# Issuing 22 small GpSimd DMAs of a two-layer trunk ahead of the constants instead of behind the fourth weight chunk

## The reference

```python
cs = silu(c)
for i in range(2):
    mod = cs @ w_mod[i] + b_mod[i]                      # 1024 x 6144: six vectors of 1024
    sh_m, sc_m, g_m, sh_f, sc_f, g_f = split(mod, 6)
    h = rmsnorm(x, norm_mix[i]) * (1 + sc_m) + sh_m
    y = hybrid_ab(h, ...) if i == 0 else multiscale_pool(h, ...)
    x = x + g_m * y
    h = rmsnorm(x, norm_ffn[i]) * (1 + sc_f) + sh_f
    x = x + g_f * hier_moe(h, w_gr[i], b_gr[i], w_er[i], b_er[i], w_gate[i], w_up[i], w_down[i])
return rmsnorm(x, norm_out)
```

## Time and profile before

| | |
|---|---|
| median of three executions | 904.04 us |
| the profiled execution | 904.04 us |
| its span, first to last instruction | 902.3 us |
| TensorE (PE) busy | 768.5 us, 85% |
| VectorE (DVE), ScalarE (ACT), GpSimd (POOL) busy | 242.9, 162.8, 37.0 us |
| mean granted TensorE clock | 0.906 of full |
| SP's DMA queue (q1) | 268.22 MB, 75.2% of 16 engines' span |
| GpSimd's DMA queue (q0) | 1.02 MB, 0.6% |

### The profile page before, as it was taken

How to read it: one execution, slowest core, us unless ns; L and a number is a source line. 1 busy time by engine, 2 the same in 40 slices (tenths; PEclk the granted TensorE clock), 3 DMA queues, 4 the chain that set the end, 5 groups by cost and what they waited for, 6 DMA issues and landing times.

```text
span 902.3 us, 9000 instructions
## 1 busy us (share of the span) xinstructions
PE 768.5 (85%) x3194; PEld 380.0 (42%) x3194; DVE 242.9 (27%) x667; ACT 162.8 (18%) x331; POOL 37.0 (4%) x63
## 2 busy tenths in 40 slices
PE   3799998697587899999999969965898999999994
PEld 1486676342452233333333326454532333333331
DVE  1105323611441212121222223525322121212124
ACT  2112022301122211111111102030311121212111
POOL 4600000000200000000000000001000000000000
PEclk9598998598588999999999986875999999999998
DMA  9977277016316999999999798555199999999961
GB/s 319 340 223 271 94 280 280 0 60 251 155 40 277 374 422 420 418 400 413 417 419 421 279 374 321 183 233 222 41 375 422 418 407 423 407 420 418 412 257 46
DMA packets 62138, 269.59 MB, mean 299 GB/s; under 512 B 3950, under 2 KB 6094, under 8 KB 37536
## 3 DMA queue, kind: packets, MB, share of 16 engines
q1 hardware_dynamic: 61152, 268.22, 75.2%
q0 software_dynamic: 960, 1.02, 0.6%
HBM read 268.18 MB, written 1.05 MB: 298 GB/s over the span
## 4 chain that ended last, share of the span: by engine, by line
PE 40%; issue 33%; DMA 18%; DVE 4%; ACT 3%; SPq 2%; POOL 1%; ACTq 0%; DVEq 0%; POOLq 0%
DMA ring<-in_w_up 14%; PE bank L673 7%; PE bank L483 5%; DMA ring<-in_w_mod 4%; PE bank L425 4%; PE bank L695 3%; PE bank L443 3%; PE bank L611 3%; PE bank L544 2%; PE bank L433 1%; PE bank L471 1%; PE bank L434 1%; PE bank L649 1%; PE bank L588 1%; PE bank L750 1%
## 5 line engine op out<-in xcount | busy, mean ns | idle before, releaser
L673 PE MATMUL bank<-ring,arena 128*64 128x512 f32 x1024 | 229.0, 600 | 30.6 <-DMA ring<-in_w_up 25.6
L673 PEld LDWEIGHTS bank<-ring,arena 128*64 128x64 f32 x1024 | 82.4, 138 | 156.9 <-issue 150.1
L709 PE MATMUL bank<-arena 128*128 128x512 f32 x256 | 117.9, 604 | 0.0
L695 PE MATMUL bank<-dn_w,hT 128*64 128x512 f32 x480 | 108.8, 593 | 0.6 <-DMA dn_w<-in_w_down 0.6
L1293 DVE SCALAR_TENSOR_TENSOR hT<-hT,bank 128x256 f32<-128x256 f32 x32 | 13.5, 421 | 235.8 <-ACT hT L936 235.8
L709 PEld LDWEIGHTS bank<-arena 128*128 128x128 f32 x256 | 46.2, 190 | 71.2 <-issue 71.2
L695 PEld LDWEIGHTS bank<-dn_w,hT 128*64 128x64 f32 x480 | 40.0, 137 | 63.8 <-issue 62.1
L425 PE MATMUL bank<-ring,cs 128*32 128x512 f32 x384 | 51.9, 679 | 13.8 <-DMA ring<-in_w_mod 13.1
L483 PE MATMUL bank<-hT,ring 128*128 128x256 f32 x192 | 47.4, 413 | 2.9 <-ACT hT L804 2.9
L936 ACT ACTIVATE hT<-bank 128x256 f32<-128x256 f32 x32 | 12.3, 383 | 188.6 <-PE bank L673 188.6
L929 ACT COPY arena<-arena 128x512 f32 x68 | 42.3, 622 | 16.7 <-issue 14.4
(11 more groups left out here) (255 smaller groups left out, 643.5 us busy)
## 6 DMA issues: line engine op xcount, KB each, us to landing
ring<-in_w_gate SPq DMA_DIRECT2D x32, 2048.0 KB, 12.8
ring<-in_w_up SPq DMA_DIRECT2D x32, 2048.0 KB, 17.3
dn_w<-in_w_down SPq DMA_DIRECT2D x30, 2048.0 KB, 9.4
ring<-in_w_mod SPq DMA_DIRECT2D x24, 2048.0 KB, 16.3
ring<-in_w_in SPq DMA_DIRECT2D x4, 2048.0 KB, 9.2
ring<-in_w_o SPq DMA_DIRECT2D x2, 2048.0 KB, 13.0
ring<-in_w_down SPq DMA_DIRECT2D x2, 2048.0 KB, 13.9
x_res<-in_x SPq DMA_DIRECT2D x2, 512.0 KB, 4.1
```

The source lines that it names most:

```text
L673: ins = pe.matmul(bank[2][h * WIN:(h + 1) * WIN, :], xw[:, b, h, k, :], w[:, h, :, k, :], start=(k == 0), stop=(k == KT - 1))
L695: ins = pe.matmul(bank[n][h * WIN:(h + 1) * WIN, :], actT[:, t, h * WIN:(h + 1) * WIN], w[:, h, t, n * HALF:(n + 1) * HALF], start=(t == 0 ...
L709: ins = pe.matmul(bank[4 + 2 * n + t][:, :], ct[:, b, t * P:(t + 1) * P], y_s[:, b, n * HALF:(n + 1) * HALF], start=(isinstance(p, int) an ...
```

## The change

The 14 and the 8 small transfers are issued directly behind `power(0)`, ahead of the other constants. The wait for chunk 3 goes away with the place that it guarded. `power(0)` keeps its place behind the four early transfers. Sources, destinations and semaphores of all transfers are as before, and no other engine's stream changes.

```diff
-            for dst, src in ((bias_col[:, 0], ...), (gain_col[:, 0], ...), (kvg[:], ...),
-                             (wkv[:, 0, :], w_kv_up[0])):
-                pool.dma_start(dst, src, allow_slow_non_contiguous=True).then_inc(S["early_in"], 16)
-            power(0)
+            for n, (dst, src) in enumerate(((bias_col[:, 0], ...), (gain_col[:, 0], ...), (kvg[:], ...),
+                             (wkv[:, 0, :], w_kv_up[0]),
+                             ... the 14 pairs that stood below ...)):
+                pool.dma_start(dst, src, allow_slow_non_contiguous=True).then_inc(S["early_in" if n < EARLY else "small_in"], 16)
+                if n == EARLY - 1:
+                    power(0)
+            for l in range(L):
+                for dst, src in (... the 4 pairs of layer l ...):
+                    pool.dma_start(dst, src).then_inc(S["late_in"], 16)
             done(pool.memset(row_sel[:], 0.0))
...
             pool.sem_inc(S["consts"], 1)

-            pool.wait_ge(chunk_in[3], 16)
-            for dst, src in (... 14 pairs ...):
-                pool.dma_start(dst, src, allow_slow_non_contiguous=True).then_inc(S["small_in"], 16)
-            for l in range(L):
-                for dst, src in (... 4 pairs ...):
-                    pool.dma_start(dst, src).then_inc(S["late_in"], 16)
             pool.wait_ge(S["kv_ms"], 1)
```

More of the change, by code:

```diff
@@ L337, in power @@
                 pool.tensor_tensor(stat[:, 4:6], stat[:, 2:4], mhalf[:], ALU.pow).then_inc(S["inv_rms"], 1)
-            for dst, src in ((bias_col[:, 0], b_mod[0].rearrange("(v p k) -> p v k", v=6, k=KT)),
+            for n, (dst, src) in enumerate(((bias_col[:, 0], b_mod[0].rearrange("(v p k) -> p v k", v=6, k=KT)),
                              (gain_col[:, 0], norm_mix[0].rearrange("(p k) -> p k", k=KT)),
                              (kvg[:], kv_norm[0].rearrange("(p o) -> p o", o=1)),
-                             (wkv[:, 0, :], w_kv_up[0])):
-                pool.dma_start(dst, src, allow_slow_non_contiguous=True).then_inc(S["early_in"], 16)
@@ L344, in _ @@
-            power(0)
+                             (wkv[:, 0, :], w_kv_up[0]),
+                             (rows[0:1], b_mod[0:1, 2 * D:3 * D]), (rows[1:2], b_mod[0:1, 5 * D:6 * D]),
+                             (rows[2:3], b_mod[1:2, 2 * D:3 * D]), (rows[3:4], b_mod[1:2, 5 * D:6 * D]),
+                             (rows[4:5], pool_scale[0:1]), (rows[5:6], norm_out.rearrange("(o d) -> o d", o=1)),
+                             (rows[6:7], norm_mix[1:2]), (rows[7:9], b_mod[1, 0:2 * D].rearrange("(v d) -> v d", v=2)),
@@ new lines, in _ @@
+                             (ws_raw, w_s[0].rearrange("g i j -> i g j")),
+                             (bias_col[:, 1], b_mod[1].rearrange("(v p k) -> p v k", v=6, k=KT)),
+                             (gain_col[:, 1], norm_ffn[0].rearrange("(p k) -> p k", k=KT)),
+                             (gain_col[:, 2], norm_ffn[1].rearrange("(p k) -> p k", k=KT)),
+                             (sgug[:], sgu_norm[0].rearrange("(g p) -> p g", p=P)),
+                             (bsb, b_s[0].partition_broadcast(P)))):
@@ new lines, in _ @@
+                pool.dma_start(dst, src, allow_slow_non_contiguous=True).then_inc(S["early_in" if n < EARLY else "small_in"], 16)
+                if n == EARLY - 1:
+                    power(0)
+            for l in range(L):
+                for dst, src in ((wroute[:, l, :, 0:NG], w_gr[l].rearrange("(p k) n -> p k n", k=KT)),
+                                 (wroute[:, l, :, NG:RCOLS], w_er[l].rearrange("(p k) n -> p k n", k=KT)),
+                                 (broute[:, l, 0:NG], b_gr[l].partition_broadcast(P)),
+                                 (broute[:, l, NG:RCOLS], b_er[l].partition_broadcast(P))):
+                    pool.dma_start(dst, src).then_inc(S["late_in"], 16)
```

## The result

| | before | after |
|---|---|---|
| median of 20 executions each | 907.79 us | 914.64 us |
| lowest and highest | 902.05, 915.57 | 908.78, 922.14 |
| ratio | | 1.0076 (95%: 1.0049 to 1.0102) |
| profiled execution, its span | 904.04, 902.3 | 918.24, 916.5 |
| mean granted clock in it | 0.906 | 0.891 |

The change costs 6.9 us, with an interval of 4.4 to 9.3. The two profiled executions lie 14.2 us apart, which is twice the cost of the change. So first the part that the change made, and then what else differs between two single profiles.

A forecast was written before the change was run, and what follows sets the result against it. The bound was TensorE's chain, waiting on DMA until chunk 2 of `w_mod` at 24.8 us. Base 904.0, removed wait 0, later constants 0 and moved transfers 5.9 summed to 909.9 us, range 905.8 to 912.6.

The forecast's parts named there:

- The waits: GpSimd's wait for chunk 3 and the later constants: nobody waits for them or the small transfers, so both cost 0.
- Where the traffic goes, and who pays: q0's traffic moves to 14.1 to 29.1 us; chunk 2 pays all 5.9 us, chunk 3 keeps 2.2 us slack.
- The price of 5.9 us: Weights queue q1 beside the 22 transfers: throughput lost at the old place, 5.9 us, delays chunk 2 to 30.7.
- 4.1 for engine time held: Middle bound of the price: 28.6% of 15 us held by q0 at a full share of 105.1%.
- C: Rival, bytes only: engines fit small packets between large ones, chunk 2 is 2.4 us late, 906.4 us; chance 0.10.
- B: Rival: chunk 2 only 2.8 us late, chunk 3 lands at 36.4 and becomes the bound, 907.7 us; chance 0.14.
- about 245 GB/s: Sign in the queues: q1's rate beside q0 between 14 and 29 us, instead of 387.
- The check by the four early transfers: At 8 to 12 us, four small transfers of 0.09 MB cost q1 1.1 us, in line with 22 at 5.9.
- D, the clock gives it back: Rival: full clock at chunks 2 and 3 and early "qi" gains 5.7 us, giving 904.2 us; chance 0.04.
- E: Rival: the small transfers are delayed somewhere until the weights are through, so 904.0 us; chance 0.03.
- 904.0 + 0 + 0 + 5.9: Whole kernel: profiled time, 0 for the wait, 0 for later constants, 5.9 for moved transfers, 909.9 us.
- plus or minus 2 us: TensorE's clock: one more or one less piece of half clock, such as that costing "qi" some 2.1 us.

The follow-up runs named there:

- the 8 alone: Against the kernel before, only the 8 late_in transfers go ahead of the constants, the 14 stay behind the wait for chunk 3; ratio 1.0044 (1.0015 to 1.0072).
- the thin router: Changed kernel with the router's weights loaded as one run per partition and copied into place by GpSimd later; ratio 1.0038 (0.9996 to 1.0081).
- the variant whose traffic lies 6 us later: Kernel before with only the wait for chunk 3 taken away, GpSimd's order kept with constants first; ratio 1.0053 (1.0010 to 1.0095).
- the load in place of the small ones: Kernel before, small transfers unmoved, with SyncE issuing 1.93 MB more ahead of chunk 2; ratio 1.0049 (1.0016 to 1.0081).
- The 14 alone: Against the kernel before, only the 14 small_in transfers go ahead of the constants, the 8 stay behind the wait; ratio 1.0044 (1.0014 to 1.0075).
- the four moved back: Kernel before with the four early transfers issued behind a wait for chunk 2; ratio 0.9988 (0.9950 to 1.0027).

## Why the direction was right and the time wrong

*The waits.* Right. Nobody waited for the small transfers, for `consts` at 2 or for GpSimd. After `kv` TensorE goes on without a pause in the changed kernel too.

*Where the traffic goes, and who pays.* Right: q0 between 14 and 29 us, chunk 2 pays, chunk 3 keeps its slack.

*The price of 5.9 us.* The throughput that q1 lost was 6.0 us. Chunk 2 was 5.0 us late in one profile and 6.2 in the other. Lost throughput was the right bound to take, against 4.1 for engine time held and 2.4 for bytes: C falls by the 8 alone (2.9 us late for 0.33 MB) and by the thin router. The Trainium skill, "DMA: Bandwidth & Descriptors", section "Queues, rings and completion order", has the engines take packets from the queues in turn. The traces agree in so far as transfers that GpSimd issued from 9.6 to 23.8 us landed within 5 to 7 us, while that of chunk 2, issued at 3.6, landed at 29.8. That q1 loses more time than q0 holds doesn't follow from turns alone. In the changed kernel q0 held 4.1 us (28.9% of 15 us at a full share of 105.1%), and q1's own packets took 3.4 us of engine time per MB instead of 2.7, which is 2.2 us more for its 3.48 MB. Together this is about the 6.0 lost. In the thin router's kernel both were smaller, 3.2 us and 2.9 us per MB. Why the large packets become slower beside small ones no run here shows.

*B.* Not in this kernel: all of it reached chunk 2. It came true in the variant whose traffic lies 6 us later.

*Small errors on the way.* q1 beside q0 was given as "about 245 GB/s", but 387 x 9.1 / 15 is 235, and 232 was measured. Chunk 1 takes 1.92 us and not 2.3, so it would have been done by 24.1 and not 24.5. The clock fell at 23.4, inside the stretch read as full, and not at 24.2. The check by the four early transfers, 1.1 us, wasn't borne out by a run that could tell it from none. None of these changes the sum.

*D, the clock gives it back.* It didn't. Chunk 2 ran at half clock behind the pause, as forecast.

*E.* It fell with the first profile.

The mechanism was right, and the price nearly so. *The step that failed is the base of the sum: "904.0 + 0 + 0 + 5.9", with the clock as "plus or minus 2 us".* I took the one profiled execution, also the median of three, as the kernel's time and let only one piece of half clock more or less stand in the range. In 20 executions the kernel before has a median of 907.79, 3.75 us above. Its 80 executions beside the experiments range from 900.7 to 916.4, and the mean granted clock goes with them: a line through them has 7 us for each 0.01 of clock, with a correlation of -0.84. Bad luck had a part in it: 12 of the 80 lie at 904.04 or below, and by that share a median of three does so about once in 16 times. Counting on so few executions was the fault, and its size was chance. So 914.64 lies 2.0 us over the end of my range, 912.6. From the measured 907.8 the same sum would have given 913.7, and the same range, moved by 3.75, would have held the result. With 5.0 to 6.2 us shown at chunk 2 and 6.9 (5.4 to 8.4 over 118 executions) at the end, some 1 us is left without a place. It may be clock: the mean over all executions is 0.8948 after and 0.8984 before, but a pause of 5.6 us at half clock lowers the mean by 0.5 x 5.6 / 910 = 0.003 without costing anything beyond itself, and what remains is too small to be told from none.

The profiles point at one place where it may lie. Between chunk 2 and matmul 500 of the stream, at about 134 us, the second profile of before lost 2.5 us against the first. Both profiles of the changed kernel, the load in place of the small ones and the thin router, with chunk 2 between 3.7 and 6.2 us late, lost 2.8 to 3.1 us there. The 14 alone and the 8 alone, about 3 us late, and the four moved back lost between -0.2 and 0.3. But the kernel without the wait, whose chunk 3 was 2.8 us late, lost 2.8 from there on. The granted clock from 65 to 100 us goes with this: 0.80 in those that lost, 0.90 in the others and in the first of before. If the kernel before pays this only in part of its executions and the changed one in nearly all, the missing 1 us is there. One profile of each variant can't show that.

## What to carry to other kernels

A wait in front of small transfers may be protecting the large one that everybody waits for. Before taking it away, ask who waits for the small ones (here nobody for 20 us) and which transfer is in flight at the place to which they go, and price them by the throughput that the large queue lost at the old place, not by their bytes. And a single profile is a sample of the clock too: take the base from many executions and the price from distances in the trace, and of these expect about 1 us from one profile to the next where a transfer's landing is one end.

## What the runs showed of the hardware

- 22 small transfers of 0.93 MB cost a saturated stream of weights 6.0 us, 2.5 times what their bytes would. With an eighth of the elements in the router's weights, and the same bytes, it was 3.8 us.
- Two profiles of the same program had 169 and 195 us of half clock, and were 5.9 us apart at 250 us of the span. One had 0.90 and the other 0.80 as the mean clock from 65 to 100 us.
- Matmuls into a free bank in a pause of 3.5 us brought the next chunk from 3.64 to 1.92 us in two profiles, and no gain could be seen at the end of the kernel (ratios 1.0024 and 0.9998).
